# Ten products per layer moved from VectorE to GpSimd, and two selection steps taken into the indexer, in a two-layer hybrid decoder trunk

## The reference, cut to what matters

```python
for l in range(DEPTH):                              # DEPTH = 2
    h = rms_norm(x, attn_norm[l])
    x = x + token_mix(h, ...)                       # projection, GLA | DSA | MLA, output projection
    h = rms_norm(x, mlp_norm[l])
    x = x + squared_relu_mlp(h, w_up[l], w_down[l])

# GLA, per chunk of 64 tokens (b: running sum of log decays)
q_dec = qc * (DK ** -0.5) * jnp.exp(b)
k_inv = kc * jnp.exp(-b)
k_end = kc * jnp.exp(b_end - b)
# DSA: an indexer score per (query, key); each query keeps its 128 best keys
score = einsum('bqhs,bqh->bqs', relu(iq . ik), iw);  _, idx = lax.top_k(score, 128)
# MLA: the last 32 of 96 rows of each query and key are turned
rotary(x, pos) = concat(x1 * cos - x2 * sin, x2 * cos + x1 * sin)
```

## Time and profile before

| | |
|---|---|
| time, median of 3 runs | 1255.13 us (1254.95 to 1256.62) |
| the profiled execution, its own time | 1253.49 us |
| its span in the trace | 1251.7 us |
| busy in the span: TensorE / VectorE / ScalarE / GpSimd | 1236.5 / 777.6 / 528.5 / 216.7 us |
| granted TensorE clock, mean | 0.999 |

### The profile page before, as it was taken

One profiled execution on the slowest core, in us unless ns is written; L12 is line 12 of the kernel. 1 busy time (PEld: TensorE's weight loads), 2 busy tenths in 40 slices (PEclk: granted clock), 3 DMA queues, 4 the chain that ended last, 5 costly groups with the idle time before them and its releaser, 6 DMA issues.

```text
span 1251.7 us, 17687 instructions
## 1 busy us (share of the span) xinstructions
PE 1236.5 (99%) x5956; PEld 973.0 (78%) x5956; DVE 777.6 (62%) x1234; ACT 528.5 (42%) x858; POOL 216.7 (17%) x140
## 2 busy tenths in 40 slices
PE   8999999999999999999999999999999999999998
PEld 7766776688888888888886667767888888888887
DVE  6699988644644554544757999785446445445444
ACT  5674438643323224224437643585442242232331
POOL 1132330020120110210522234200201102102002
PEclk9999999999999999999999999999999999999999
DMA  6212220023232223322322222201232232233223
GB/s 242 89 51 68 68 85 2 17 102 116 99 101 91 95 98 101 101 84 101 101 89 81 68 68 68 69 2 46 89 101 90 96 101 101 84 101 101 95 98 109
DMA packets 30720, 108.36 MB, mean 87 GB/s; under 512 B 3536, under 2 KB 3536, under 8 KB 30672
## 3 DMA queue, kind: packets, MB, share of 16 engines
q1 hardware_dynamic: 29520, 103.82, 24.9%
q0 software_dynamic: 432, 2.86, 0.6%
q10 hardware_dynamic: 720, 1.07, 0.3%
HBM read 105.64 MB, written 2.10 MB: 86 GB/s over the span
## 4 chain that ended last, share of the span: by engine, by line
PE 82%; DVE 11%; issue 4%; ACT 3%; DMA 1%; ACTq 0%; DVEq 0%
PE bank L898 19%; PE bank L897 19%; PE bank L899 19%; PE bank L517 4%; PE bank L518 4%; PE bank L519 4%; PE bank L540 2%; PE bank L538 2%; PE bank L539 2%; PE bank L779 1%; PE bank L791 1%; DVE sel L1401 1%; PE bank L806 1%; DVE sel L1354 1%; DVE m L1350 1%
## 5 line engine op out<-in xcount | busy, mean ns | idle before, releaser
L952 ACT ACTIVATE wh<-raw 128x1024 fp32r<-128x1024 f32 x191 | 201.7, 1056 | 377.9 <-PE bank L899 246.5
L1275 DVE TENSOR_TENSOR wl<-raw,wh 128x1024 fp32r<-128x1024 f32 x155 | 240.5, 1552 | 75.6 <-ACT wh L952 75.5
L897 PE MATMUL bank<-hh,wl 128*128 128x512 f32 x512 | 200.0, 391 | 0.0
L897 PE MATMUL bank<-xmh,wl 128*128 128x512 f32 x512 | 199.3, 389 | 0.0
L899 PE MATMUL bank<-hl,wh 128*128 128x512 f32 x512 | 199.2, 389 | 0.0
L899 PE MATMUL bank<-xml,wh 128*128 128x512 f32 x512 | 199.2, 389 | 0.0
L898 PE MATMUL bank<-xmh,wh 128*128 128x512 f32 x512 | 199.2, 389 | 0.0
L898 PE MATMUL bank<-hh,wh 128*128 128x512 f32 x512 | 199.2, 389 | 0.0
L482 POOL TENSOR_TENSOR x<-x,rsb 128x512 f32<-128x512 f32 x62 | 82.0, 1322 | 587.4 <-DVE rsb L1696 587.4
L1685 DVE TENSOR_TENSOR sqb<-tf 128x512 f32<-128x512 f32 x64 | 44.3, 692 | 181.6 <-ACT hh L1238 181.6
L517 PE MATMUL bank<-xgh,wl 128*128 128x512 f32 x368 | 151.0, 410 | 2.7 <-DVE xgl L1288 2.5
(11 more groups left out here) (218 smaller groups left out, 1669.2 us busy)
## 6 DMA issues: line engine op xcount, KB each, us to landing
raw<-in_stream SPq DMA_DIRECT2D x191, 512.0 KB, 3.3
out_y<-x SPq DMA_DIRECT2D x8, 256.0 KB, 3.5
x<-in_x ACTq DMA_DIRECT2D x4, 256.0 KB, 7.0
x<-in_x SPq DMA_DIRECT2D x4, 256.0 KB, 7.1
con<-in_consts POOLq DMA_DIRECT2D x1, 976.5 KB, 5.2
par<-in_params POOLq DMA_DIRECT2D x1, 916.0 KB, 5.5
par<-in_params POOLq DMA_DIRECT2D x1, 896.0 KB, 6.9
raw<-in_stream SPq DMA_DIRECT2D x2, 256.0 KB, 4.1
```

Source lines behind the costliest of these rows:

```text
L897: pe.matmul(B.t[s][:], wl[:, s, n_block(k)], src_h[:, k], start=(k == 0), stop=False)
L952: act.activation(wh[:, s], raw[:, s], ACT.Copy).then_inc(hi_ready.sem, 1)
L1275: vec.tensor_tensor(wl[:, s], raw[:, s], wh[:, s], ALU.subtract).then_inc(lo_ready.sem, 1)
```

## The change

On GpSimd's side, three new helpers are called inside its loop over the units, always behind the low part: `scale_decay` (four products of 128 x 512: `e1` by `rb` into `kinv` and `e2` by `rb` in place, for both pairs), `turn_query` (four products of 32 x 512: the rotary rows by `cos`, after which GpSimd waits for its own product), and `key_end` (two of 128 x 512, with the decay broadcast over each chunk). VectorE loses these ten instructions, and waits for the new semaphores `scaled` and `q_turned` in their place. The GLA scale 64 ** -0.5 goes into the two products that make `gqp`, which become scalar-tensor-tensor instructions.

The order of selection steps is now a list, `SELECT`, which begins with two steps of block 3 alone. These two stand in slot 7, before and after `weighted(3)`. The slots 12 to 15 have three steps instead of two, and the slots 19 to 22 have 4, 4, 3, 2 instead of 5, 5, 5, 4. The total stays 48.

```diff
+SELECT = [3, 3] + [3, 2, 1] * (TOPK // 8 - 2) + [2, 1] * 2
...
+        q_turned = S("q_turned", H)
+        scaled = S("scaled", 4)
...
+                def scale_decay(buf, pr):
+                    pool.wait_ge(*exp_ready.at(l, 1))
+                    src, dst = (e1, kinv) if buf == 0 else (e2, e2)
+                    pool.tensor_tensor(dst[:, pr], src[:, pr], rb[:], ALU.mult).then_inc(scaled.sem, 1)
+
+                def turn_query(h, ahead):
+                    pool.wait_ge(*ahead)
+                    pool.wait_ge(*q_copied.at(l, h))
+                    pool.tensor_tensor(tf[64:QK, h % 2], tf[64:QK, h % 2], cos, ALU.mult).then_inc(q_turned.sem, 1)
+                    pool.wait_ge(*q_turned.at(l, h))
+
+                def key_end(pr):
+                    pool.wait_ge(*B.freed(l, f"gk{pr}"))
+                    dec = e1[:, pr].rearrange("p (c t) -> p c t", t=CHUNK)[:, :, CHUNK - 1:CHUNK]
+                    pool.tensor_tensor(tf[:, pr].rearrange("p (c t) -> p c t", t=CHUNK),
+                                       kinv[:, pr].rearrange("p (c t) -> p c t", t=CHUNK),
+                                       dec.to_broadcast([P, NCHUNK, CHUNK]), ALU.mult).then_inc(kend_ready.sem, 1)
...
                     pool.tensor_tensor(wl[:, u % 2], raw[:, u % 2], wh[:, u % 2], ALU.subtract)\
                         .then_inc(lo_ready.sem, 1)
+                    if u == 9:
+                        pool.wait_ge(const_loaded, 16)
+                        scale_decay(0, 0)
+                        scale_decay(0, 1)
+                        turn_query(0, scaled.at(l, 1))
+                    if u in (10, 11):
+                        scale_decay(1, u - 10)
+                        turn_query(u - 9, scaled.at(l, u - 8))
+                    if u == 12:
+                        turn_query(3, lo_ready.at(l, u + AHEAD))
+                    if u in (14, 15):
+                        key_end(u - 14)
...
                 def select_steps(first, n):
-                    for i0 in range(first, first + n, 3):
-                        queries = [3 - i % 3 for i in range(i0, min(i0 + 3, first + n))]
+                    rest = SELECT[first:first + n]
+                    while rest:
+                        queries = rest[:3] if len(set(rest[:3])) == len(rest[:3]) else rest[:1]
+                        rest = rest[len(queries):]
...
                 def mla_turn(h):
                     vec.wait_ge(*q_copied.at(l, h))
-                    vec.tensor_tensor(tf[64:QK, h % 2], tf[64:QK, h % 2], cos, ALU.mult)
...
                 def mla_queries(h):
                     vec.wait_ge(*B.freed(l, f"mq{h}"))
+                    vec.wait_ge(*q_turned.at(l, h))
...
                     if u in (12, 13):
-                        vec.wait_ge(*exp_ready.at(l, pr))
+                        vec.wait_ge(*scaled.at(l, pr))
                         vec.wait_ge(*zeroed.at(l, 0))
-                        link(vec.scalar_tensor_tensor(kinv[:, pr], rb[:], GLA_DK ** -0.5, e1[:, pr],
-                                                      ALU.mult, ALU.mult))
                         vec.wait_ge(*B.filled(l, f"gq{pr}"))
-                        vec.tensor_tensor(gqp[0:64, 2 * pr], B[f"gq{pr}"][0:64, :], kinv[0:64, pr], ALU.mult)
-                        vec.tensor_tensor(gqp[64:P, 2 * pr + 1], B[f"gq{pr}"][64:P, :], kinv[64:P, pr], ALU.mult)\
-                            .then_inc(*B.on_read(f"gq{pr}"))
+                        vec.scalar_tensor_tensor(gqp[0:64, 2 * pr], B[f"gq{pr}"][0:64, :], GLA_DK ** -0.5,
+                                                 kinv[0:64, pr], ALU.mult, ALU.mult)
+                        vec.scalar_tensor_tensor(gqp[64:P, 2 * pr + 1], B[f"gq{pr}"][64:P, :], GLA_DK ** -0.5,
+                                                 kinv[64:P, pr], ALU.mult, ALU.mult).then_inc(*B.on_read(f"gq{pr}"))
                     if u in (14, 15):
-                        link(vec.tensor_tensor(e2[:, pr], e2[:, pr], rb[:], ALU.mult))
+                        vec.wait_ge(*scaled.at(l, 2 + pr))
...
                     if u == 7:
+                        select_steps(0, 1)
                         weighted(3)
+                        select_steps(1, 1)
...
                     if u in (14, 15):
-                        vec.wait_ge(*B.freed(l, f"gk{pr}"))
-                        dec = e1[:, pr].rearrange("p (c t) -> p c t", t=CHUNK)[:, :, CHUNK - 1:CHUNK]
-                        vec.tensor_tensor(tf[:, pr].rearrange("p (c t) -> p c t", t=CHUNK),
-                                          kinv[:, pr].rearrange("p (c t) -> p c t", t=CHUNK),
-                                          dec.to_broadcast([P, NCHUNK, CHUNK]), ALU.mult)\
-                            .then_inc(kend_ready.sem, 1)
                         mla_keys(pr)
-                per_slot = {9: 3, 10: 3, 11: 3, 12: 2, 13: 2, 14: 2, 15: 2, 16: 4, 17: 4, 18: 4,
-                            19: 5, 20: 5, 21: 5, 22: 4}
-                done = 0
+                per_slot = {9: 3, 10: 3, 11: 3, 12: 3, 13: 3, 14: 3, 15: 3, 16: 4, 17: 4, 18: 4,
+                            19: 4, 20: 4, 21: 3, 22: 2}
+                done = 2
```

## The result

The changed kernel takes 1248.18 us (median of 4 runs, 1247.98 to 1248.70), the kernel before 1255.84 us beside it (4 runs, 1254.95 to 1256.62). The ratio is 0.9938, with a 95% interval of 0.9922 to 0.9954: 7.7 us or 0.62% faster. The prediction said faster, but 1250.7 with 1249.3 to 1255.4.

A forecast was written before the change was run, and what follows sets the result against it. TensorE, busy 1236.5 of 1251.7 us, was taken as the bound; removing its 2.19 us wait for `mk1` in both layers saves 4.4 us, taking the median from 1255.13 to 1250.7, range 1249.3 to 1255.4.

The forecast's parts named there:

- What bounds it, and the path to `mk1`: TensorE waits 2.19 us a layer at L618 until VectorE's L1389 frees `mk1`; freed by 129.7 to 131.6, the wait goes.
- The race at the port: Slot 10: VectorE's L1362 starts 0.07 us before GpSimd's low part at their shared port, saving 1.54 us of waiting.
- Rival (a): VectorE loses both 0.07 us races at the port; about 0.4 us a layer is gained, 1254.3 us; chance 0.24.
- The sum alone: VectorE's work without port waits: 6.9 - 0.3 - 4.1 = 2.5 us a layer saved, against 2.2 needed.
- Slots 8 and 9, and the alternation: Slot 8's L1401 held up 1.2 us, slot 9 gains nothing; VectorE waits for one GpSimd instruction, not a row.
- rival (b): From slot 10, GpSimd keeps the port between instructions; TensorE waits some 1.3 us longer a layer, 1257.7 us; chance 0.08.
- The selection steps: One more step each in slots 12 to 15 costs 4.1 us; slot 7's two fill VectorE's idle gaps, costing nothing.
- the sum: The L618 wait of 2.19 us goes in both layers, 4.4 us; median 1255.13 becomes 1250.7; chance 0.63.
- the wait's price: Removing TensorE's wait at L618 is worth its 2.19 us a layer, 4.4 us in all.
- The range's low end: 1249.3 us, if other short waits vanish, and for the runs' spread of 1.7 us.

The follow-up runs named there:

- The two late kernels: Changed kernel with a 0.17 us VectorE memset ahead of the two-input product: in slots 10 and 11, 1252.26 us; in slot 10 alone, 1248.31 us.
- the kernel with four products: Changed kernel with only the four query products on GpSimd, decays and key ends back on VectorE: 1248.01 us, ratio 0.9945.
- the one with the steps alone: Kernel before with only the selection steps moved and all ten products left on VectorE: 1260.04 us, ratio 1.0041.
- the execution of 1255.28 us: Kernel before, unchanged, profiled once more: 1255.28 us.
- the 49 executions above: Runs of the unchanged kernel before beside the experiments: 9 at 1253.2 to 1253.7 us, the others at 1254.7 to 1258.4; median 1254.99.
- the six runs: Runs of the kernel before with only the selection steps moved, no product moved: median 1260.04 us.
- slots 10 and 11 late: Changed kernel with a 0.17 us VectorE memset ahead of the two-input product in slots 10 and 11: 1252.26 us, ratio 0.9975.
- six products: Changed kernel with only decays and key ends on GpSimd, the four query products back on VectorE: 1252.11 us, ratio 0.9977.

## Why the prediction was wrong

**What bounds it, and the path to `mk1`: right.** The wait at L618 was the whole stage's loss, and it went in both layers.

**The race at the port: right, to the hundredth.** L1362 was forecast at 91.39 ahead of a low part at 91.46; they came at 91.40 and 91.48. The two late kernels show that this order, not the sum of work, decides: 0.17 us of delay in two slots costs 4.2 us. Rival (a)'s order came out when it was brought about, but its time, 1254.3, was 2.0 us too long, 1.6 of it by the same term as the forecast's (below): 1252.26 was measured. The sum alone (2.5 us saved against 2.2 needed) would have given the same verdict for the wrong reason. It would also have ruled out the kernel with four products, which takes 4.1 us less off VectorE and is as fast.

**Slots 8 and 9, and the alternation: right.** The last L1401 took 0.93 us longer (1.2 forecast), and L1400 of slot 9 ended at 85.46, as before. GpSimd's product behind a held-up VectorE instruction took 1.75 instead of 1.30 us: they do take turns, and rival (b) has nothing behind it here. The 32-row and broadcast products cost 1.06 to 1.10 us, a little less than the 1.29 taken.

**The selection steps: nearly right as a cost, needless as a part.** Slot 7's two steps filled the gaps. Between the kernel before and the one with the steps alone, the third step adds 0.7 to 1.25 us a slot, 3.7 in slots 12 to 15 of layer 0, where 4.1 were taken.

**The step that failed is the sum.** It had two terms wrong. First, the wait's price. The sum took 2.19 us a layer; `mv1` starts 2.60 us earlier. The rest is in small pieces. The idle time in brackets counts from the recorded end of the matmul before, but matmuls overlap: in the execution of 1255.28 us, one that starts at 132.60 has its end at 132.99, while the next could start 0.23 us after it, at 132.83. That hides 0.16 us. `mv0` had a small wait too, and starts 0.18 us earlier after, 0.05 of it from the start of the run. And each `mla_v` behind a wait is recorded with 1.13 instead of 1.03 us. With the same in layer 1 this gives 5.3 us of span instead of 4.4. Second, and larger, "1251.7 us of span (1253.49 of its own time), 1.6 below the median; [...] and the median 1255.13 becomes 1250.7". This carried the 1.6 us between the profiled execution and the median over as if it were a constant. It was itself a cost of the wait: by the levels, the clock fell behind one wait or both in 40 of the 49 executions above, for some 1.7 us each. The changed kernel's median lies on its profiled time (1248.18 and 1248.19). Against the 1255.13 from which the forecast started, the gain is 6.95 us: 5.3 from the waits and 1.65 from the clock, where the sum had 4.4 and nothing. So of the 2.5 us by which 1250.7 was missed, 0.9 are the first term and 1.6 the second. The other 0.7 us of the measured 7.7 are a matter of the draw: the four runs of the kernel before have a median of 1255.84, between two of its levels, and 49 runs have 1254.99.

**The bounds.** The range's low end allowed for the spread of the runs as noise. The spread was 1.7 us in three runs, with the profile below all of them, which should have raised the question of what the other executions had in them; the page's clock line, in tenths, can't show it.

## What to carry to other kernels

When an engine's work is taken off it, ask first which of its instructions are held up by a neighbour: savings ahead of such an instruction are lost, until the start moves ahead of the neighbour's, and then the whole wait goes at once. So what counts is the order of two starts: here four products of 32 x 512 were worth as much as all ten, and the six larger ones by themselves 2.7 us. And when a kernel's median lies above its profiled execution and its runs fall on levels, look at the mean clock of each run before taking the difference for noise: an idle gap of TensorE can cost more than its own length.

## What was unexpected of the hardware

An idle stretch of TensorE of 2.2 us, in an otherwise full stream of matmuls, is followed in some executions by 3.4 us at half clock, and in others of the same kernel not; with 3.8 us of idle, the six runs all had a clock of 0.996 or 0.997, and in one wait of the profiled one it fell before the wait was over and stayed low for 6.8 us; with waits of 1.6 us (slots 10 and 11 late) or 1.1 and 0.4 us (six products), none of 18 runs was below 0.999. What decides from one execution to the next stays open.
